# Sums of expert outputs moved behind six of eight weight rows, and the next gather behind the first expert's second layer

## The chip, the cores and the metric

One NeuronCore of a Trainium2 chip runs the whole kernel. The metric is the device time of one execution in microseconds (us). Before the change it is 1108.04 us, the median of 3 runs (1106.1 to 1108.91).

## The reference

One step of a one-layer decoder trunk on 304 tokens (256 prompt tokens, 32 sample tokens, 16 meta tokens). A mixer (RG-LRU, convolution module and gated linear attention side by side, behind one input and one output projection) is followed by a mixture of 32 experts, of which each of the 288 remaining tokens uses four. The change lies in the mixture:

```python
def expert_block(args):
    xb, e = args
    hid = xb @ lp["moe_w1"][e] + lp["moe_b1"][e]          # 1024 x 2048
    gate = jnp.minimum(hid[:, :D_FF], SWIGLU_LIMIT)
    lin = jnp.clip(hid[:, D_FF:], -SWIGLU_LIMIT, SWIGLU_LIMIT)
    act = gate * jax.nn.sigmoid(SWIGLU_ALPHA * gate) * (lin + 1.0)
    return act @ lp["moe_w2"][e] + lp["moe_b2"][e]        # 1024 x 1024
...
rows = out[dest] * gates.reshape(-1)[order][:, None]
y = jax.ops.segment_sum(rows, tok, num_segments=n)
```

The output of the mixture is added to the layer's input and normalised. All data are float32, so the weights of the experts are 12 MiB each, 384 MiB in all.

## The kernel before

The mixer and the routing take the first 173 us. Then the experts run in 16 pairs. Pairs 0 and 1 are the "first" group, pairs 2 to 13 run in a loop, two pairs to an iteration, and pairs 14 and 15 are the "last" group; pair 15 is also called final. Each expert takes up to 64 tokens (the capacity), so the two experts of a pair, called j = 0 and j = 1, share matrices of 128 columns.

**The ring of weights.** SyncE's queue loads the weights into a ring of eight slots of 2 MiB, called pieces here (`load_group`, L492). A pair uses twelve pieces: 12n to 12n+3 for the first layer of j = 0 in pair n, the next four for that of j = 1, then two each for their second layers. In the first and last groups each piece is a DMA of its own; in the loop the first-layer pieces go two by two, as units of 4 MiB. An issue of piece k waits until TensorE has counted `w_used` to k - 7 (`room`, L497; a unit waits for its second piece). TensorE counts `w_used` up behind every second k step of a first layer (L1939) and every fourth of a second layer (L1955), always after one piece.

**TensorE's order in a pair** (`pair`, L1918) is written out by hand:
1. first layer of j = 0 (`first_layer`, L1919; 8 k steps, banks 0 and 1), with the gather of the upper half of the pair's tokens (`gather(1)`, L1890, bank 5) between k = 2 and k = 3;
2. sums 0 and 1 (`combine`, L1898): the outputs of the pair before, `eout`, are spread over the tokens by a matmul with `putT`, into banks 6 and 7. There are five such sums, into banks 6, 7, 5, 2 and 4, and VectorE adds each to the running result (`add_part`, L1390), which counts `y_added`;
3. the biases of j = 1 (`biases`, L1796, matmuls at L1793), which open banks 0 and 1 again and wait until VectorE has read them (`g1_ready`, `l1_ready`, written by L1428 and L1429);
4. sums 2 to 4;
5. first layer of j = 1, with the transposes of j = 0's activations (`inner`, L1957, L1961) between k = 3 and k = 4;
6. the next pair's `gather(0)` into bank 2 and its biases of j = 0; in the final pair two `residual` matmuls (L1915) instead;
7. transposes of `put` (L2009), the matrix that places and weighs the outputs of the pair;
8. second layer of j = 0 (`second_layer`, L1941, matmuls at L1951) with `inner(1)` in its middle, then that of j = 1.

**VectorE's order in a pair**: move the gathered tokens (L1377), build `pick` and `bsel`, activate j = 0 (L1428 to L1434: two reads of the banks, two products), the five additions, `make_put(0)` (L1439), `bsel` (L1324), activate j = 1, `make_put(1)`, move the next gather's result, copy half of the outputs (L1445). ScalarE computes the sigmoid (L918) and copies transposed tiles and the other half of the outputs.

In the code a wait is `eng.wait_ge(semaphore, count)`. An engine works through its own instructions in the order written. The two places around the change, before it:

```python
pe.wait_ge(bsel_ready, 2 * pi + 2)
pe.wait_ge(g1_ready, 2 * pi + 1)
pe.wait_ge(l1_ready, 2 * pi + 1)
biases(1)
```

Of the kernel before, what the change touches and what calls it, by code (L numbers as in the profile page):

```python
# [23 lines left out]
P = 128  # L24
D = 1024
KT = D // P
# [42 lines left out]
NCOMB = 5  # L69
# [48 lines left out]
def build_kernel(nc, x_prompt, x_sample, state_conv_a, state_rglru, state_conv_b, state_gla, meta_tokens, ln0_g, ln0_b,  # L118
# [4 lines left out]
    with ExitStack() as ctx:  # L123
# [14 lines left out]
        ident = sb("ident", [P, P])  # L138
# [125 lines left out]
        put = late(3, 2 * CAP)  # L264
# [40 lines left out]
        bank = [ctx.enter_context(nc.psum_tensor(f"bank{n}", [P, 512], F32)) for n in range(8)]  # L305
# [50 lines left out]
        pick_ready, bsel_ready, put_ready = sem("pick_ready"), sem("bsel_ready"), sem("put_ready")  # L356
        gather_full, xT_ready = sem("gather_full"), sem("xT_ready")
# [602 lines left out]
        def _(dve):  # L960
# [361 lines left out]
            def make_bsel(e, j):  # L1322

                dve.tensor_scalar(bsel[0:2 * NE, j, :], ones[0:2 * NE, 0:CAP], selx[0:2 * NE, bass.ds(e, 1)], None, ALU.mult  # L1324
                                  ).then_inc(bsel_ready, 1)
# [95 lines left out]
            with dve.Fori(0, n_pass) as r:  # L1421
                with dve.Fori(0, NE // GROUP) as g:
                    for q in range(2):
                        pi = r * PAIRS + 2 * g + q
                        def activate(j):
                            n, e = 2 * pi + j, GROUP * g + 2 * q + j
                            dve.wait_ge(w_used, PAIR * pi + W1P * j + W1P)
                            dve.tensor_scalar(g1[:, :], bank[0][:, :], LIMIT, None, ALU.min).then_inc(g1_ready, 1)  # L1428
                            dve.tensor_scalar(l1[:, :], bank[1][:, :], LIMIT, -LIMIT, ALU.min, ALU.max).then_inc(l1_ready, 1)  # L1429
                            dve.wait_ge(l1_ready, n + 1)  # L1430
                            dve.scalar_tensor_tensor(l1[:, :], l1[:, :], 1.0, g1[:, :], ALU.add, ALU.mult).then_inc(t_done, 1)
                            dve.wait_ge(t_done, n + 1)
                            dve.wait_ge(sg_ready, n + 1)
                            dve.tensor_tensor(l1[:, :], l1[:, :], sg[:, :], ALU.mult).then_inc(act_ready, 1)  # L1434

                        def make_put(j):
                            n, e = 2 * pi + j, GROUP * g + 2 * q + j
                            for t in range(3):
                                ins = dve.tensor_scalar(put[:, t, j * CAP:(j + 1) * CAP], io64[:, :], posm[:, t, bass.ds(n, 1)],  # L1439
                                                        gates[:, t, bass.ds(e, 1)], ALU.is_equal, ALU.mult)  # L1440
                            ins.then_inc(put_ready, 1)

                        def expert_out(j):
                            dve.wait_ge(w_used, PAIR * pi + 2 * W1P + 2 * j + 2)
                            dve.tensor_copy(eout[64 * j:64 * j + 64, 1, :], bank[OUT_BANK[j]][64:128, :]).then_inc(out_ready, 1)  # L1445

                        e0 = GROUP * g + 2 * q
                        dve.wait_ge(gather_full, 2 * pi + 5)
                        batch_out(q, 1)
                        make_pick(2 * pi + 2)  # L1450
                        make_bsel(e0 + 1, 1)
                        activate(0)
                        for c in range(NCOMB):
                            add_part(c, NCOMB * pi)
                        make_put(0)
                        make_bsel(e0 + 2, 0)
                        activate(1)
                        make_put(1)
                        dve.wait_ge(gather_full, 2 * pi + 6)
                        batch_out(1 - q, 0)  # L1460
                        expert_out(0)
                        expert_out(1)
# [58 lines left out]
        def _(pe):  # L1521
# [274 lines left out]
            def biases(j):  # L1796

                bias_bank(j, 0)
                bias_bank(j, 1)
# [98 lines left out]
            def combine(pi, c):  # L1898

                out = bank[COMB_BANK[c]]  # L1900
                if c == 0:
                    for q in range(4):
                        ins = pe.matmul(out[SAMP * q:SAMP * q + SAMP, 0:QD], putT[:, 2 * P:2 * P + SAMP],  # L1903
                                        eout[:, q // 2, (q % 2) * QD:(q % 2 + 1) * QD], start=True, stop=True)
                    ins.then_inc(comb_full, 1)
                    return
                t, h = divmod(c - 1, 2)
                pe.matmul(out[:, :], putT[:, t * P:(t + 1) * P], eout[:, h, :], start=True, stop=True).then_inc(comb_full, 1)  # L1908

            def residual(c):  # L1910

                if c == 4:
                    pe.matmul(bank[LAST_BANK[c]][:, 0:QD], ident[:, :], Yq[:, :], start=True, stop=False)
                else:
                    pe.matmul(bank[LAST_BANK[c]][:, :], ident[:, :], Y[:, c // 2, c % 2 * 512:(c % 2 + 1) * 512],  # L1915
                              start=True, stop=False)

            def pair(q, gi, pi, first=False, final=False, group=""):  # L1918
                def first_layer(j, k0, k1):  # L1919

                    for k in range(k0, k1):
                        f = (PAIR * q + W1P * j) // 2 + k // 4
                        if k % 4 == 0:
                            pe.wait_ge(w_full[f % 4], 16 * (gi * 3 + f // 4 + 1))
                        if k % 4 == 2 and group == "first":
                            pe.wait_ge(w_half[f % 4], 16 * (f // 4 + 1))
                        if k % 4 == 2 and group == "last":
                            pe.wait_ge(w1_half_last[f % 4], 16 * (f // 6 + 1))
                        if j == 0 and k < 4 and first:
                            pe.wait_ge(xT_first, k + 1)  # L1930
                        elif j == 0 and k % 4 == 0:
                            pe.wait_ge(xT_ready, 2 * pi + k // 4)
                        for b in range(2):
                            for h in range(2):
                                c = f % 4 * 2 * SLOT + k % 4 * MB1 + (2 * b + h) * 512
                                ins = pe.matmul(bank[b][64 * h:64 * h + 64, :], xT[:, q, k, j * CAP:(j + 1) * CAP],  # L1936
                                                ring[:, c:c + 512], start=False, stop=k == KT - 1)
                        if k % 2 == 1:
                            ins.then_inc(w_used, 1)  # L1939
# [36 lines left out]
                else:  # L1976
                    first_layer(0, 3, KT)

                pe.wait_ge(putT_ready, pi + 1)
                pe.wait_ge(out_ready, 4 * pi + 1)  # L1980
                combine(pi, 0)
                combine(pi, 1)
                pe.wait_ge(bsel_ready, 2 * pi + 2)
                pe.wait_ge(g1_ready, 2 * pi + 1)
                pe.wait_ge(l1_ready, 2 * pi + 1)
                biases(1)
                pe.wait_ge(xT_ready, 2 * pi + 1)
                for c in range(2, NCOMB):
                    combine(pi, c)
                first_layer(1, 0, 4)  # L1990
                inner(0)
                first_layer(1, 4, KT)

                if final:
                    pe.wait_ge(y_added, NCOMB * pi + NCOMB)
                    residual(0)
                    residual(1)
                else:
                    pe.wait_ge(pick_ready, pi + 3)
                    pe.wait_ge(y_added, NCOMB * pi + 4)  # L2000
                    gather(0)
                    pe.wait_ge(bsel_ready, 2 * pi + 3)
                    pe.wait_ge(g1_ready, 2 * pi + 2)
                    pe.wait_ge(l1_ready, 2 * pi + 2)
                    biases(0)
                pe.wait_ge(put_ready, 2 * pi + 2)
                pe.wait_ge(actT_ready, 2 * pi + 1)
                for t in range(3):
                    ins = pe.transpose(bank[3][:, t * P:(t + 1) * P], put[:, t, :], ident[:, :])  # L2009
                    if final and t == 0:  # L2010
                        ins.then_inc(gather_full, 1)
                ins.then_inc(putT_full, 1)
                pe.wait_ge(y_added, NCOMB * pi + NCOMB)
                second_layer(0, 0, 4)
                pe.wait_ge(putT_ready, pi + 2)
                inner(1)
                if final:
                    pe.wait_ge(xT_ready, 2 * pi + 2)
                    residual(4)
                second_layer(0, 4, KT)  # L2020
                pe.wait_ge(actT_ready, 2 * pi + 2)
                second_layer(1, 0, KT)

# [60 lines left out]
```

## Time and profile before

| what | before |
|---|---|
| median of 3 runs | 1108.04 us (1106.1 to 1108.91) |
| the profiled execution | 1106.05 us |
| its span, first to last instruction | 1104.3 us |
| TensorE busy | 1071.1 us (97%) |
| VectorE busy | 374.0 us (34%) |
| ScalarE busy | 163.5 us (15%) |
| moved by DMA | 425.77 MB, 386 GB/s over the span |
| mean granted TensorE clock | 0.993 of full speed |

The page of the profile has the span in 40 slices, each 27.6 us long. In them a digit is the busy share of an engine in tenths. Busy time of TensorE is that of a pipelined engine, so it does not say how fast it works; the timeline (instructions in order of time, those of one line merged) and the windows (busy time, granted clock and DMA rate of a stretch) say more. Matmuls in float32 have two records each. In a row of the timeline, "x24" is the number of records, and the bracket gives idle time of the engine ahead of it and what ended that.

### The profile page before, as it was taken

How to read it: one execution, taken by the hardware profiler on the slowest of the kernel's cores; microseconds unless marked ns; L12 is line 12 of the kernel's file. 1: busy time of each engine (PE TensorE's matmuls, PEld its weight loads, DVE VectorE, ACT ScalarE, POOL GpSimd, SP SyncE). 2: the span in 40 equal slices, each digit the busy share in tenths (PEclk: the TensorE clock that was granted, in tenths of full speed). 3: DMA queues.
4: the chain of work that ended last, by engine and by line, in shares of the span. 5: the costliest groups of instructions: out<-in, count | busy, mean ns of one | idle time of the engine just before them, and what ended most of it. 6: DMA issues, size and time to landing. Idle time of an engine off the chain costs nothing.

```text
span 1104.3 us, 13732 instructions
## 1 busy us (share of the span) xinstructions
PE 1071.1 (97%) x5411; PEld 464.0 (42%) x5411; DVE 374.0 (34%) x939; ACT 163.5 (15%) x314; POOL 44.2 (4%) x103
## 2 busy tenths in 40 slices
PE   7999999999999999999999999999999999999996
PEld 4667554434333343334333333333334343434332
DVE  4797665313131414141413122323231312222134
ACT  4264633000000010001000101010101010010002
POOL 8000210000000000000000000000000000000001
PEclk9999999999999999999999999999999999999998
DMA  9533549999999999999999999999999999999993
GB/s 297 197 151 160 232 166 358 402 426 426 414 439 425 431 433 428 430 432 431 425 438 424 434 429 434 427 436 425 434 428 434 432 431 430 424 429 427 427 428 150
DMA packets 34878, 425.77 MB, mean 386 GB/s; under 512 B 5865, under 2 KB 12398, under 8 KB 16409
## 3 DMA queue, kind: packets, MB, share of 16 engines
q1 hardware_dynamic: 32961, 423.62, 91.1%
q0 software_dynamic: 1888, 1.75, 0.6%
q8 instruction: 20, 0.33, 0.1%
q14 instruction: 9, 0.07, 0.0%
HBM read 423.39 MB, written 2.17 MB: 385 GB/s over the span
## 4 chain that ended last, share of the span: by engine, by line
PE 76%; DMA 21%; DVE 2%; issue 0%; ACT 0%; SPq 0%; DVEq 0%
PE bank L1936 36%; DMA ring<-in_moe_w_dram 21%; PE bank L1951 10%; PE bank L1536 7%; PE bank L1895 6%; PE bank L1908 6%; PE bank L1763 3%; PE bank L1793 2%; PE bank L1563 1%; PE bank L1961 1%; PE bank L1541 1%; PE bank L1903 1%; PE bank L1785 0%; PE bank L2009 0%; PE bank L1756 0%
## 5 line engine op out<-in xcount | busy, mean ns | idle before, releaser
L1936 PE MATMUL bank<-ring,hT 128*64 128x512 f32 x2048 | 457.2, 599 | 12.6 <-DMA ring<-in_moe_w_dram 12.5
L1936 PEld LDWEIGHTS bank<-ring,hT 128*64 128x64 f32 x2048 | 143.2, 137 | 297.8 <-issue 282.8
L1951 PE MATMUL bank<-ring 128*64 128x512 f32 x1024 | 226.8, 595 | 0.0
L1428 DVE TENSOR_SCALAR ring<-bank 128x512 f32<-128x512 f32 x32 | 22.1, 691 | 311.8 <-PE bank L1936 311.8
L1951 PEld LDWEIGHTS bank<-ring 128*64 128x64 f32 x1024 | 70.7, 137 | 132.8 <-issue 130.6
L1445 DVE COPY ring<-bank 64x512 f32<-64x512 f32 x32 | 22.2, 694 | 218.9 <-PE bank L1951 218.9
L1895 PEld LDWEIGHTS bank<-ring 128*128 128x128 f32 x744 | 85.4, 192 | 25.1 <-issue 25.1
L1895 PE MATMUL bank<-ring 128*128 128x128 f32 x744 | 91.3, 279 | 0.0
L1377 DVE TENSOR_SCALAR hT<-bank,ring 128x128 f32<-128x128 f32 x128 | 43.6, 401 | 129.7 <-PE bank L1895 129.3
L918 ACT ACTIVATE ring<-ring 128x512 f32<-128x512 f32 x32 | 20.1, 629 | 379.3 <-DVE ring L1428 379.3
L1908 PE MATMUL bank<-ring 128*128 128x512 f32 x128 | 63.5, 618 | 0.0
L922 ACT ACTIVATE ring<-bank 128x512 f32<-128x512 f32 x32 | 19.1, 597 | 248.4 <-PE bank L1961 248.4
L1536 PE MATMUL bank<-hT,ring 128*128 128x304 f32 (+1 forms) x208 | 55.1, 424 | 0.0
L1390 DVE TENSOR_TENSOR xt<-xt,bank 128x512 f32<-128x512 f32 x64 | 43.9, 685 | 5.8 <-PE bank L1908 5.5
L1536 PEld LDWEIGHTS bank<-hT,ring 128*128 128x128 f32 x208 | 40.1, 195 | 13.2 <-issue 0.4
L933 ACT ACTIVATE ring<-bank 64x512 f32<-64x512 f32 x32 | 18.9, 589 | 148.8 <-PE bank L1951 148.8
L667 POOL TENSOR_TENSOR ring<-ring 128x256 f32<-128x256 f32 x1 | 0.7, 722 | 943.1 <-ACT ring L946 943.1
L1908 PEld LDWEIGHTS bank<-ring 128*128 128x128 f32 x128 | 21.7, 189 | 34.9 <-issue 34.9
L1793 PE MATMUL bank<-ring 32*64 32x512 f32 x256 | 35.9, 613 | 0.0
L1763 PE MATMUL bank<-ring 128*128 128x512 f32 x64 | 29.2, 602 | 0.0
L1961 PEld LDWEIGHTS bank<-ident,ring 128*128 128x128 f32 x128 | 18.0, 210 | 26.0 <-issue 26.0
L1439 DVE TENSOR_SCALAR ring<-io,ring 128x64 f32<-128x64 f32 x96 | 24.1, 307 | 0.0
(327 smaller groups left out, 616.8 us busy)
## 6 DMA issues: line engine op xcount, KB each, us to landing
ring<-in_moe_w_dram SPq DMA_DIRECT2D x96, 2048.0 KB, 28.4
ring<-in_moe_w_dram SPq DMA_DIRECT2D x48, 4096.0 KB, 27.6
ring<-in_w_in_dram SPq DMA_DIRECT2D x5, 1536.0 KB, 13.5
ring<-in_w_out_dram SPq DMA_DIRECT2D x2, 2048.0 KB, 10.9
ring<-in_w_in_dram SPq DMA_DIRECT2D x1, 2048.0 KB, 13.3
xt<-in_x_prompt_dram SPq DMA_DIRECT2D x2, 512.0 KB, 3.7
lnbc<-in_ln_g_dram SPq DMA_DIRECT2D x2, 512.0 KB, 12.2
lnbc<-in_ln_b_dram SPq DMA_DIRECT2D x2, 512.0 KB, 12.5
```

Source lines behind the costliest of these rows:

```text
L1377: ins = dve.tensor_scalar(xT[:, parity, 4 * b + k, :], bank[(2, 5)[b]][:, k * 2 * CAP:(k + 1) * 2 * CAP], ln1c[:, 0, 4 * b + k:4 * b + k + ...
L1390: dve.tensor_tensor(dst, dst, bank[COMB_BANK[c]][:, :], ALU.add).then_inc(y_added, 1)
L1439: ins = dve.tensor_scalar(put[:, t, j * CAP:(j + 1) * CAP], io64[:, :], posm[:, t, bass.ds(n, 1)], gates[:, t, bass.ds(e, 1)], ALU.is_equa ...
L1445: dve.tensor_copy(eout[64 * j:64 * j + 64, 1, :], bank[OUT_BANK[j]][64:128, :]).then_inc(out_ready, 1)
L1536: ins = pe.matmul(out, a, b, start=n == 0, stop=n == len(pairs) - 1)
L1763: ins = pe.matmul(bk(f"P{t}{c}")[:, :], yT[:, k, cols[t][0]:cols[t][1]], wout[:, k, c * 512:(c + 1) * 512], start=k == 0, stop=k == KT - 1)
L1793: pe.matmul(bank[b][64 * h:64 * h + 64, :], bsel[e0:e0 + NE, j, :], b1_sb[e0:e0 + NE, h, :], start=True, stop=False)
L1895: ins = pe.matmul(out, xh[:, t, k * P:(k + 1) * P], pick[:, t, :], start=t == 0, stop=t == 2)
L1908: pe.matmul(out[:, :], putT[:, t * P:(t + 1) * P], eout[:, h, :], start=True, stop=True).then_inc(comb_full, 1)
L1936: ins = pe.matmul(bank[b][64 * h:64 * h + 64, :], xT[:, q, k, j * CAP:(j + 1) * CAP], ring[:, c:c + 512], start=False, stop=k == KT - 1)
L1951: ins = pe.matmul(bank[OUT_BANK[j]][64 * h:64 * h + 64, :], actT[:, j, k % 4, (k // 4) * CAP:(k // 4 + 1) * CAP], ring[:, c:c + 512], star ...
L1961: ins = pe.transpose(bank[3][:, k * P:(k + 1) * P], l1[:, k:512:4], ident[:, :])
```

## The change

On VectorE, `make_put(1)` moves ahead of the activation of j = 1. On TensorE, in every pair but the final one, all five sums move behind k = 5 of the first layer of j = 1, as one run; in the final pair they stay where they were. In the first group (pairs 0 and 1) the transposes of `put` move into the middle of the first half of j = 0's second layer, and the next pair's `gather(0)` and biases move from ahead of j = 0's second layer to behind it. No instruction that computes is added or dropped.

```diff
                         for c in range(NCOMB):
                             add_part(c, NCOMB * pi)
                         make_put(0)
+                        make_put(1)
                         make_bsel(e0 + 2, 0)
                         activate(1)
-                        make_put(1)
                         dve.wait_ge(gather_full, 2 * pi + 6)
...
-                pe.wait_ge(putT_ready, pi + 1)
-                pe.wait_ge(out_ready, 4 * pi + 1)
-                combine(pi, 0)
-                combine(pi, 1)
+                def combined(c0, c1):
+                    if c0 == 0:
+                        pe.wait_ge(putT_ready, pi + 1)
+                        pe.wait_ge(out_ready, 4 * pi + 1)
+                    else:
+                        pe.wait_ge(xT_ready, 2 * pi + 1)
+                    for c in range(c0, c1):
+                        combine(pi, c)
+
+                late_sums = not final
+                if not late_sums:
+                    combined(0, 2)
                 pe.wait_ge(bsel_ready, 2 * pi + 2)
                 pe.wait_ge(g1_ready, 2 * pi + 1)
                 pe.wait_ge(l1_ready, 2 * pi + 1)
                 biases(1)
+                if not late_sums:
+                    combined(2, NCOMB)
                 pe.wait_ge(xT_ready, 2 * pi + 1)
-                for c in range(2, NCOMB):
-                    combine(pi, c)
                 first_layer(1, 0, 4)
                 inner(0)
-                first_layer(1, 4, KT)
...
+                if late_sums:
+                    first_layer(1, 4, 6)
+                    combined(0, 2)
+                    combined(2, NCOMB)
+                    first_layer(1, 6, KT)
                 else:
+                    first_layer(1, 4, KT)
...
+                if group == "first":
+                    pe.wait_ge(y_added, NCOMB * pi + NCOMB)
+                    pe.wait_ge(actT_ready, 2 * pi + 1)
+                    second_layer(0, 0, 2)
+                    put_over()
+                    second_layer(0, 2, 4)
+                else:
+                    if final:
+                        pe.wait_ge(y_added, NCOMB * pi + NCOMB)
+                        residual(0)
+                        residual(1)
+                    else:
+                        next_gather()
+                    put_over()
+                    pe.wait_ge(y_added, NCOMB * pi + NCOMB)
+                    second_layer(0, 0, 4)
                 pe.wait_ge(putT_ready, pi + 2)
                 inner(1)
...
                 second_layer(0, 4, KT)
+                if group == "first":
+                    next_gather()
                 pe.wait_ge(actT_ready, 2 * pi + 2)
                 second_layer(1, 0, KT)
```

`next_gather()` holds the waits, `gather(0)` and `biases(0)` of step 6 as they were, and `put_over()` the waits and transposes of step 7.

## Rows read from the trace of the kernel before

**Rows 1.** The page, section 2: busy tenths in 40 slices.
```profile
PE   7999999999999999999999999999999999999996
...
DMA  9533549999999999999999999999999999999993
```

**Rows 2.** Windows: us, busy time by engine, clock, DMA share, GB/s.
```profile
199.00:202.00 3.00, 3.00 (x18) 1.00 (x15) 0.00 (x0) 0.00 (x0) 0.00 (x0) 1.00 0.61 180
...
260.00:262.00 2.00, 2.00 (x10) 0.68 (x12) 0.00 (x0) 0.60 (x1) 0.00 (x0) 1.00 1.05 336
...
480.00:1080.00 600.00, 585.76 (x2923) 229.88 (x2921) 154.62 (x381) 49.95 (x79) 0.00 (x0) 0.99 1.00 430
...
686.00:688.00 2.00, 2.00 (x6) 0.53 (x6) 0.00 (x0) 0.00 (x0) 0.00 (x0) 0.50 1.10 475
```

**Rows 3.** Timeline of TensorE, pair 1: start us, us, line, operation, records.
```profile
229.94 5.32 PE L1936 MATMUL bank<-ring,hT 128*64 128x512 f32 x24
...
246.79 0.64 PE L1903 MATMUL bank<-ring 128*32 128x256 f32 x8
247.36 1.12 PE L1908 MATMUL bank<-ring 128*128 128x512 f32 x2
248.42 1.09 PE L1793 MATMUL bank<-ring 32*64 32x512 f32 x8
249.44 2.84 PE L1908 MATMUL bank<-ring 128*128 128x512 f32 x6
252.21 7.09 PE L1936 MATMUL bank<-ring,hT 128*64 128x512 f32 x32
...
266.93 2.94 PE L1895 MATMUL bank<-ring 128*128 128x128 f32 x24
...
285.92 1.46 PE L1936 MATMUL bank<-ring,hT 128*64 128x512 f32 x6
```

**Rows 4.** Waits of TensorE: total us, times, longest us.
```profile
PE bank L1936 <- DMA ring<-in_moe_w_dram: 12.5, 8, 2.2
```

**Rows 5.** Timeline of TensorE, pair 15.
```profile
1030.23 3.65 PE L1936 MATMUL bank<-ring,hT 128*64 128x512 f32 x16
1035.04 1.94 PE L1936 MATMUL bank<-ring,hT 128*64 128x512 f32 x8 [1.16 <-DMA ring<-in_moe_w_dram]
...
1072.23 0.55 PE L2009 MATMUL bank<-ident,ring 128*128 128x128 f32 x3 [1.60 <-DVE ring L1439]
1072.71 3.65 PE L1951 MATMUL bank<-ring 128*64 128x512 f32 x16
...
1087.85 1.12 PE L1915 MATMUL bank<-xt,ident 128*128 128x512 f32 x2
```

**Rows 6.** Timeline of TensorE's weight loads, the last piece in use.
```profile
1083.98 0.14 PEld L1951 LDWEIGHTS bank<-ring 128*64 128x64 f32 x2 [0.38 <-DMA ring<-in_moe_w_dram]
```

**Rows 7.** Timeline of SyncE's DMA queue: issues of pieces 12, 18, (24, 25) and (26, 27).
```profile
199.93 0.33 SPq L514 DMA_DIRECT2D ring<-in_moe_w_dram  x1
...
226.71 0.33 SPq L514 DMA_DIRECT2D ring<-in_moe_w_dram  x1
...
259.49 0.35 SPq L510 DMA_DIRECT2D ring<-in_moe_w_dram  x1
...
267.17 12.57 SPq L510 DMA_DIRECT2D ring<-in_moe_w_dram  x2
```

**Rows 8.** Timeline of VectorE in pair 1: the two reads, a put.
```profile
246.91 0.69 DVE L1428 TENSOR_SCALAR ring<-bank 128x512 f32<-128x512 f32 x1 [6.24 <-PE bank L1936]
247.52 0.68 DVE L1429 TENSOR_SCALAR ring<-bank 128x512 f32<-128x512 f32 x1
...
252.92 0.76 DVE L1439 TENSOR_SCALAR ring<-io,ring 128x64 f32<-128x64 f32 x3
```

**Rows 9.** Timeline of TensorE behind two waits for weights.
```profile
684.21 5.35 PE L1936 MATMUL bank<-ring,hT 128*64 128x512 f32 x16 [2.25 <-DMA ring<-in_moe_w_dram]
...
917.91 5.37 PE L1936 MATMUL bank<-ring,hT 128*64 128x512 f32 x24 [2.23 <-DMA ring<-in_moe_w_dram]
```

More of the change, by code:

```diff
@@ L1986, in pair, with next_gather @@
                 biases(1)
+                if not late_sums:
+                    combined(2, NCOMB)
                 pe.wait_ge(xT_ready, 2 * pi + 1)
-                for c in range(2, NCOMB):
-                    combine(pi, c)
                 first_layer(1, 0, 4)
                 inner(0)
-                first_layer(1, 4, KT)
[L1994 to L1997, printed above, removed]
-                else:
+                if late_sums:
[3 more added lines that the diff above has]
+                    first_layer(1, 6, KT)
+                else:
+                    first_layer(1, 4, KT)
+                def next_gather():
                     pe.wait_ge(pick_ready, pi + 3)
@@ L2005, in pair, with put_over @@
                     biases(0)
[L2006 to L2014, printed above, removed]
+                def put_over():
+                    pe.wait_ge(put_ready, 2 * pi + 2)
+                    pe.wait_ge(actT_ready, 2 * pi + 1)
+                    for t in range(3):
+                        ins = pe.transpose(bank[3][:, t * P:(t + 1) * P], put[:, t, :], ident[:, :])
+                        if final and t == 0:
+                            ins.then_inc(gather_full, 1)
+                    ins.then_inc(putT_full, 1)
+                if group == "first":
+                    pe.wait_ge(y_added, NCOMB * pi + NCOMB)
+                    pe.wait_ge(actT_ready, 2 * pi + 1)
+                    second_layer(0, 0, 2)
[11 more added lines that the diff above has]
+                    second_layer(0, 0, 4)
                 pe.wait_ge(putT_ready, pi + 2)
```

## The prediction

> **What bounds the kernel now.** I read the slices of the page first: from slice 9 on TensorE and the DMA engines both stand at 9 tenths, so both are nearly full and the question is which one waits for the other [rows 1]. The stretches say it in numbers: 430 GB/s from 480 to 1080 us, and a hole before that, 180 GB/s from 199 to 202 us [rows 2]. A piece of weights is 2.097 MB, so at 430 GB/s it takes 4.88 us and the twelve pieces of a pair 58.5 us. The timeline of TensorE gives its own pace: pair 1 begins at 229.94 us and pair 2 at 285.92 us, 55.98 us with no idle time between them [rows 3]. So TensorE is the faster of the two by 2.5 us a pair. It first lives on the lead that the ring gave; in the second half it waits for weights, 8 times for 12.5 us in all, 2.2 us at most [rows 4]. From there the stream of weights sets the pace, and the end is the start of the stream, plus its bytes over its rate, plus its holes, plus the tail behind the last piece. The last piece lands at 1083.98 us, and the last second layer is done at 1087.85 us [rows 5, 6].
>
> **The holes of the stream.** The DMA queue issues a piece when a slot of the ring is free, that is when TensorE has signalled the matmuls that used it. The hole at 199 to 202 us ends with the issue of piece 12 at 199.93 us, which waits for k = 0 and 1 of expert 1's first layer in pair 0 [rows 7]. It is worth 3 x (430 - 180) / 430 = 1.74 us, so the piece before ended, counted like an issue (the latency to the first byte drops out of the differences), at 198.19. From 199.93 twelve pieces reach 258.5, and the next unit (24, 25) is issued at 259.49: 1.0 us dry. Two units later the second of the two issues that take 12.57 us from 267.17 on starts at about 279.4, where the stream is due at 279.0: 0.4 us [rows 7]. My sum is 3.1 us of holes; the stretch from 260 to 262 us shows 2 x (430 - 336) / 430 = 0.44 us where I have 1.0, so half a microsecond is what such a sum can be off by [rows 2]. After that the queue only gets longer.
>
> **The change, part by part.**
> (a) The sums move. Between the first layer of expert 0 (ends 246.79) and that of expert 1 (begins 252.21) stand today: sums 0 and 1, 1.63 us; the biases, 1.02; sums 2 to 4, 2.77 [rows 3]. In all pairs but the last the 4.40 us of sums go between k = 5 and k = 6 of expert 1's first layer. No matmul is added or removed.
> (b) What sums 0 and 1 cover. The biases of expert 1 overwrite banks 0 and 1 and wait until VectorE has read them. Those two reads start at 246.91 and end at 248.20 [rows 8]. Today that lies under sums 0 and 1, which end at 248.42. With the sums gone TensorE stands still from 246.79 until shortly behind 248.20; a release takes about 0.1 us (VectorE begins 0.12 behind TensorE's end), I take 248.26, so **1.47 us in each of 15 pairs**. The bounds: 0 if the wait were covered otherwise (nothing else is queued in front of it), 1.63 if it cost all that the sums filled. I take 1.47, which comes from two rows.
> (c) The split of the eight k steps into 6 and 2 adds a break. A run of 16 records of the layer takes 3.65 us and one of 32 takes 7.09, so a break costs up to 0.21; joining sum 1 and sums 2 to 4 into one run gives back as much (two records take 1.12, six take 2.84, so the four added cost 0.43 each, and eight 3.70, not 3.96) [rows 3, 5]. Between -0.2 and +0.2 a pair; I take 0. So a pair takes 55.98 + 1.47 = 57.45 us, still under 58.5.
> (d) Earlier room. The signals for k = 1, 3 and 5 of expert 1 come 4.40 - 1.47 = 2.93 us earlier, all later ones of the pair 1.47 us later.
> (e) VectorE. The five additions follow the sums by one; the second put is now built before the activation of expert 1 and not behind it. The adds end 0.9 us behind the sums, the two puts and the selection need 1.8 more (0.76 a put), and two k steps of matmuls last half of 7.09 us [rows 3, 8]: nothing on TensorE waits for them, and the activation begins as before. In the last pair this pays: there TensorE waits 1.60 us for the put, which stands behind the whole activation [rows 5]. That wait goes; next late would be the data.
> (f) The first group. Its second layer begins ahead of the gather and the biases (3.89 us), so the room from expert 0's second layer comes about 4 us earlier, less the 1.47 of (b), and that from expert 1's at +1.47. The gather reads nothing that is late, and the move of its result to the other buffer ends some 3 us before pair 1 or 2 reads it. No DMA changes its place in the queue.
>
> **The stream summed again**, all counted like issues. Piece 12 is issued at 199.93 - 2.93 = 197.0, before 198.19: no hole, 1.74 us gained. (Pieces not named come in time.) Piece 18 is due at 198.19 + 6 x 4.88 = 227.5 and issued at 226.71 + 1.47 = 228.2: 0.7 dry. Unit 24 is due at 257.5 and issued at 259.49 + 1.47 - 2.93 = 258.0: 0.6. Unit 26 is due at 267.8, but waits for the end of expert 1's first layer in pair 1, which is two bubbles late: 267.17 + 2.94 = 270.1, 2.3 dry [rows 7]. Unit 40, in pair 2, is due at 338.4 and issued 49.5 + 1.47 behind the pair's start (288.86), at 339.8: 1.4 dry. After it the queue grows by 1.1 us a pair. Holes 5.0 against 3.1: **the stream ends 1.9 us later**; the last piece lands at 1085.9, and with 3.87 us behind it the second layer is done at 1089.7.
>
> **TensorE summed again.** Pair 2 begins at 288.86, pair 15 at 288.86 + 13 x 57.45 = 1035.7 instead of 1030.23. Data in time: pair 13 begins at 920.8, and its weights, for which it waited until 917.91 today, are there by 919.8 [rows 9]. In the last pair 57.62 us (to 1087.85) lose the wait of 1.16 for data and that of 1.60 for the put: 54.86, so 1090.6, or 1089.9 if (c) gives back 0.05 a pair [rows 5]. TensorE now ends 2.1 to 2.75 us later, the stream 1.9. I take **+2.4 us**: 1108.5 for a profiled execution of 1106.05, and 1110.4 on the median of 1108.04. The profiled one lies 2 us under the median, within the spread of the three runs. What a measurement of this kernel can tell from no change is about 0.3%, 3.3 us, so this counts as no difference.
>
> **Rivals.**
> R1, the clock of TensorE falls behind the bubbles; slower. After a wait of 2.25 us at 684 us the granted clock stood at 0.50 (1.2 GHz) from 686 to 688, and 16 records took 5.35 us instead of 3.65, 1.70 us lost; after one of 2.23 at 918 us 24 records took 5.37 us, as 24 do in pair 1 (5.32), so the clock stayed at 2.4 GHz [rows 2, 3, 5, 9]. The shorter wait of 1.60 us left the 16 records behind it at 3.65 us [rows 5]. If it fell in every pair, 57.45 + 1.70 = 59.15 is over 58.5 and TensorE is some 25 us late, 1135; in half of them +12, 1122. Chance 0.08. The Trainium skill speaks against the change here: "TensorE: Matmul & The Clock Gate", section "A second HAM failure mode: psum-queue depth-cycling", says that small idle times between groups of matmuls, when frequent, make the clock swing between its levels. By that rule the time would be R1's. This trace agrees with it only for one wait of 2.25 us; the one of 1.60 does not bear it out.
> R2, the bubble is the mechanism but longer, or the added break is not paid back; slower. There is no slack: every 0.1 us a pair is 1.3 us at the end, and from 0.07 us more a pair the total is over 3.3 us. With 0.2 (the upper end of c): 13 x 0.2 = 2.6 on top, 1113. Chance 0.23.
> R3, the stream alone sets the end, TensorE is some tenths a pair quicker than summed: +0.5 to +1.9, 1109.2. Chance 0.19; with my forecast's 0.40 it shares the verdict.
> R4, a gain. The hole at 200 us goes and the bubbles cost the stream nothing, because the latency before data hides 1 or 2 us: -1.74, and 0.4 at the end, 1106. Chance 0.10, of which 0.06 for over 0.3%: there is less idle time in the stream (3.1 us) than that would take.
>
> **How the numbers follow.** Slower by over 0.3%: R1 and most of R2, 0.30. Faster by over 0.3%: 0.06. Within: 0.64. The range reaches from R4's 1106 to just beyond R2, 1114.5; R1 is left out.
>
> **What the profile would show.** TensorE idle about 1.5 us in front of the biases (L1793) in 15 pairs, released by VectorE's L1429; a pair start every 57.4 us; waits for weights nearly gone (12.5 us before); no wait of 1.6 us for the put at the end; the hole at 199 to 202 us gone, new ones near 270 and 340 us. I would be wrong if pairs still started every 58.4 us with waits for weights (R3, R4), or if the clock row showed 0.5 behind the bubbles (R1).

## The result, and the profile after

The changed kernel takes 1117.87 us (median of 4 runs, 1116.95 to 1120.55), beside 1107.35 us for the kernel before, which was run once more with it. The ratio is 1.0097, with a 95% interval of 1.0079 to 1.0115: **slower by about 1%, some 10 us.** The forecast was 1110.4 us and a range up to 1114.5.

| what | before | after |
|---|---|---|
| profiled execution | 1106.05 us | 1116.95 us |
| its span | 1104.3 us | 1114.1 us |
| mean granted TensorE clock | 0.993 | 0.989 |
| TensorE's waits for weights | 12.5 us, 8 times | none |
| its waits in front of the biases of j = 1 | none | 22.2 us, 15 times |

First the waits of TensorE (total, times, longest), which answer to [rows 4]:

```profile
PE bank L1793 <- DVE ring L1429: 22.2, 15, 1.5
PE bank L1541 <- DMA ring<-in_ln_b_dram: 6.3, 1, 6.3
PE bank L1541 <- ACT xt L692: 1.6, 2, 1.2
PE bank L1785 <- ACT hT L864: 0.3, 1, 0.3
```

One kind of wait has taken the place of the other. L1429 is VectorE's second read of the banks. Next TensorE's timeline of pair 1 and of the start of pair 2, beside [rows 3]:

```profile
239.68 8.80 PE L1936 MATMUL bank<-ring,hT 128*64 128x512 f32 x40
249.96 1.09 PE L1793 MATMUL bank<-ring 32*64 32x512 f32 x8 [1.48 <-DVE ring L1429]
250.98 7.09 PE L1936 MATMUL bank<-ring,hT 128*64 128x512 f32 x32
258.00 0.75 PE L1961 MATMUL bank<-ident,ring 128*128 128x128 f32 x4
258.68 3.65 PE L1936 MATMUL bank<-ring,hT 128*64 128x512 f32 x16
262.26 0.64 PE L1903 MATMUL bank<-ring 128*32 128x256 f32 x8
262.83 3.70 PE L1908 MATMUL bank<-ring 128*128 128x512 f32 x8
...
289.19 5.32 PE L1936 MATMUL bank<-ring,hT 128*64 128x512 f32 x24
```

The bubble is 1.48 us long, the five sums stand between k = 5 and 6, and pair 2 begins at 289.19 us, 3.3 us later than before. From here 13 pairs of 57.48 us would reach pair 15 at 1036.4. It begins later:

```profile
1043.27 5.32 PE L1936 MATMUL bank<-ring,hT 128*64 128x512 f32 x24
...
1080.26 1.98 PE L1915 MATMUL bank<-xt,ident 128*128 128x512 f32 x4
1082.08 0.49 PE L2024 MATMUL bank<-ident,ring 128*128 128x128 f32 x3
1082.50 3.65 PE L1951 MATMUL bank<-ring 128*64 128x512 f32 x16
...
1087.20 10.52 PE L1951 MATMUL bank<-ring 128*64 128x512 f32 x48
1097.66 1.12 PE L1915 MATMUL bank<-xt,ident 128*128 128x512 f32 x2
```

Pair 15 is 13.04 us late against [rows 5] and then wins 3.23 us back (54.39 us instead of 57.62: no wait for data, no wait for the put). The second layer is done 9.81 us late, which is the whole difference of the spans. The 6.8 us between 1036.4 and 1043.27 are in rows like these, TensorE behind two of the 15 bubbles, and two windows (us, busy time by engine, granted clock, DMA share, GB/s) at the first:

```profile
422.57 1.09 PE L1793 MATMUL bank<-ring 32*64 32x512 f32 x8 [1.48 <-DVE ring L1429]
423.59 8.77 PE L1936 MATMUL bank<-ring,hT 128*64 128x512 f32 x32
...
654.20 1.09 PE L1793 MATMUL bank<-ring 32*64 32x512 f32 x8 [1.48 <-DVE ring L1429]
655.21 8.78 PE L1936 MATMUL bank<-ring,hT 128*64 128x512 f32 x32
```

```profile
422.00:426.00 4.00, 3.43 (x14) 1.00 (x16) 1.81 (x3) 0.49 (x1) 0.00 (x0) 0.70 1.03 438
424.00:426.00 2.00, 2.00 (x6) 0.47 (x4) 0.00 (x0) 0.00 (x0) 0.00 (x0) 0.50 1.04 442
```

32 records of the first layer take 8.77 us and not 7.09, and the granted clock is 0.50 from 424 to 426 us: it has fallen to 1.2 GHz, and later it comes back to 2.4. In windows of 2 us over the whole stretch of the experts falls of the clock begin at 422, 654, 828 and 1002 us, each time directly behind a bubble. The shortfall adds up to 6.84 us, and the four pairs in question are 59.2 us long instead of 57.5. Before, there were two falls, behind waits for weights at 684 and 801 us. The rows of [rows 9] have the first; this is the second, where 24 records take 7.07 us and not 5.32:

```profile
801.05 7.07 PE L1936 MATMUL bank<-ring,hT 128*64 128x512 f32 x24 [2.23 <-DMA ring<-in_moe_w_dram]
```

They cost the kernel nothing: TensorE had time in hand there, and the pairs that begin at 684.21 and 801.05 us are 58.41 and 58.43 us long, like those beside them (58.43 and 58.44).

The stream of weights, beside [rows 2]:

```profile
199.00:202.00 3.00, 3.00 (x18) 1.21 (x16) 0.00 (x0) 0.60 (x1) 0.00 (x0) 1.00 1.02 437
...
262.00:280.00 18.00, 18.00 (x87) 7.27 (x86) 7.33 (x16) 2.31 (x4) 0.00 (x0) 1.00 0.93 383
338.00:344.00 6.00, 6.00 (x30) 2.01 (x28) 0.69 (x1) 0.59 (x1) 0.00 (x0) 1.00 0.88 341
```

The hole at 200 us is gone. The missing rate is that below 430 GB/s: one hole of 18 x 47 / 430 = 2.0 us has come near 270 us, and one of 6 x 89 / 430 = 1.2 us near 340 us, where the forecast had 2.3 and 1.4.

### The profile page after: what moved, and what is told of

Read it like the earlier page. It is cut to its first block, busy times and chain, and to the rows that moved or that the text cites. A ratio compares the mean times of both kernels' runs of the same rounds, so it can differ in the third digit from the quotient of the medians.

```text
span 1114.1 us, 13742 instructions
## 1 busy us (share of the span) xinstructions
PE 1073.1 (96%) x5411; PEld 466.1 (42%) x5411; DVE 377.8 (34%) x939; ACT 164.1 (15%) x314; POOL 44.3 (4%) x103
## 4 chain that ended last, share of the span: by engine, by line
PE 96%; DVE 2%; issue 1%; DMA 0%; ACT 0%; DVEq 0%
PE bank L1936 41%; PE bank L1951 20%; PE bank L1895 8%; PE bank L1536 7%; PE bank L1908 5%; PE bank L1793 3%; PE bank L1763 3%; PE bank L1961 2%; PE bank L1563 1%; DVE ring L1429 1%; PE bank L1541 1%; PE bank L1903 1%; PE bank L2024 1%; PE bank L1785 0%; PE bank L1756 0%
## 5 line engine op out<-in xcount | busy, mean ns | idle before, releaser
L1936 PE MATMUL bank<-ring,hT 128*64 128x512 f32 x2048 | 463.3, 603 | 0.0
L1445 DVE COPY ring<-bank 64x512 f32<-64x512 f32 x32 | 22.2, 693 | 208.7 <-PE bank L1951 208.7
L1386 DVE TENSOR_TENSOR ring<-ring,bank 128x256 f32<-128x256 f32 x16 | 6.7, 421 | 182.3 <-PE bank L1903 182.3
L1908 PE MATMUL bank<-ring 128*128 128x512 f32 x128 | 59.5, 606 | 0.0
L1793 PE MATMUL bank<-ring 32*64 32x512 f32 x256 | 35.8, 611 | 22.2 <-DVE ring L1429 22.2
L1536 PEld LDWEIGHTS bank<-hT,ring 128*128 128x128 f32 x208 | 39.1, 190 | 12.5 <-issue 0.4
L1763 PE MATMUL bank<-ring 128*128 128x512 f32 x64 | 29.2, 601 | 0.0
## 6 DMA issues: line engine op xcount, KB each, us to landing
lnbc<-in_ln_g_dram SPq DMA_DIRECT2D x2, 512.0 KB, 12.5
```

The source lines that it names most:

```text
L1536: ins = pe.matmul(out, a, b, start=n == 0, stop=n == len(pairs) - 1)
L1763: ins = pe.matmul(bk(f"P{t}{c}")[:, :], yT[:, k, cols[t][0]:cols[t][1]], wout[:, k, c * 512:(c + 1) * 512], start=k == 0, stop=k == KT - 1)
L1793: pe.matmul(bank[b][64 * h:64 * h + 64, :], bsel[e0:e0 + NE, j, :], b1_sb[e0:e0 + NE, h, :], start=True, stop=False)
```

## The experiments

Nine kernels ran, one of them in two sets (cover and cover_again), in five rounds each beside the kernel before. The kernel before had medians of 1106.3 to 1106.7 us in those. "Falls" are stretches of the profiled execution with a granted clock under 1, from 180 us to the end of the last second layer (some 8 us or more behind it, in the last microseconds, the clock is at 0.50 in every kernel). The mean granted clock of a whole execution, which each run has, says that the profiled executions are no exceptions: 0.985 to 0.989 in the four of the changed kernel, 0.986 to 0.990 in late_only, 0.984 to 0.989 in split_bias, but 0.992 to 0.996 in the 12 of fill and 0.992 to 0.997 in the 11 of half_fill.

| label | usual pair, us | idle before the biases, us | falls | median us | ratio to before (95%) |
|---|---|---|---|---|---|
| before | 55.98 | none | 2 | 1106.5 | 1 |
| the change | 57.48 | 1.48 | 4 | 1117.87 | 1.0097 (1.0079 to 1.0115) |
| fill | 57.53 | none | 0 | 1109.64 | 1.0027 (1.0016 to 1.0039) |
| half_fill | 57.49 | 0.85 | 0 | 1109.05 | 1.0025 (1.0012 to 1.0038) |
| late_only | 57.49 | 1.48 | 4 | 1118.47 | 1.0112 (1.0094 to 1.0131) |
| split_bias | 57.38 | 0.89 | 4 | 1116.29 | 1.0090 (1.0072 to 1.0109) |
| half_cover | 56.92 | 0.92 | 0 | 1107.73 | 1.0004 (0.9991 to 1.0018) |
| cover | 56.13 | none | 0 | 1105.25 | 0.9987 (0.9976 to 0.9999) |
| cover_again | 56.13 | none | 1 | 1105.32 | 0.9990 (0.9978 to 1.0001) |
| cover_old_first | 56.13 | none | 1 | 1106.38 | 0.9998 (0.9987 to 1.0009) |
| put_only | 55.98 | none | 2 | 1106.02 | 0.9997 (0.9985 to 1.0008) |
| first_only | 55.98 | none | 3 | 1108.89 | 1.0019 (1.0005 to 1.0033) |

The usual pair is the distance between the starts of two pairs where TensorE waits for no weights and the clock stays up.

**Work in the bubble.** Against the changed kernel:

```diff
                 if not late_sums:
                     combined(0, 2)
+                else:
+                    pe.wait_ge(putT_ready, pi + 1)
+                    pe.wait_ge(out_ready, 4 * pi + 1)
+                    pe.matmul(bank[3][:, :], ident[:, :], xh[:, 0, 0:512], start=True, stop=True)
+                    pe.matmul(bank[3][:, 0:320], ident[:, :], xh[:, 0, 0:320], start=True, stop=True)
```

Expected:

> The changed kernel, with two matmuls that nobody reads (512 and 320 columns of the normalised rows against the identity, into bank 3) in front of the biases of expert 1 in the 15 pairs that have the bubble. They last about 1.4 us, so TensorE works through the time in which it otherwise waits 1.48 us for VectorE; the pair stays as long as it is, 57.5 us. Theory (the bubble of 1.48 us makes TensorE the only bound, +2.75 us, and the granted clock falls behind some of these idle times, four times 1.7 us in the profiled run): the clock stays at full in every pair, pair 15 starts near 1036.5 us, the run takes 1109.5 to 1111, some 7 us less than the changed kernel. Rival (the clock falls for another reason, such as the run of sums inside the layer or the time of day of the fall, and idle time has no part in it): still four or so falls, 1117 to 1118.

Measured: 1109.64 us. Useless work in the place of idle time, and some 8 us are gone. TensorE's timeline in pair 1:

```profile
252.02 1.12 PE L1995 MATMUL bank<-ring,ident 128*128 128x512 f32 x2
252.98 0.70 PE L1996 MATMUL bank<-ring,ident 128*128 128x320 f32 x2
253.61 1.09 PE L1793 MATMUL bank<-ring 32*64 32x512 f32 x8
```

(This execution begins pair 1 at 235.16 us, 3.6 us later than the changed kernel: in the mixer, ahead of 180 us, its clock lost 5.1 us and not 1.7. It also waits 1.4 us for weights near the end. So its total of 1114.78 us is over the median, and pair 15 starts at 1042.2 us, not near 1036.5.) The pair is as long as with the bubble, and no window between 180 and 1096 us has a clock under 1. So the pair's length and the clock are separate costs, and the clock's falls come with the idle time. The rival, that idle time has no part in them, is refuted: the run of sums inside the layer is there in fill too.

**Half of the bubble filled.** As above, but one matmul of 256 columns instead of the two.

> The changed kernel with one matmul that nobody reads (256 columns of the normalised rows against the identity, bank 3, about 0.5 us) in front of the biases of expert 1 in 15 pairs: the pair stays 57.5 us long, since VectorE's reads decide when the biases start, but TensorE's idle time is about 0.9 to 1.0 us in place of 1.48. Theory (half_cover had no falls because its idle time is 0.9 us next to full-array work, and split_bias had four because its idle time of 0.9 us is followed by 1.5 us of bias matmuls instead of 1.0): no falls, 1109 to 1111, as with the full filling. Rival (a pair paced by TensorE falls with any idle time of about 0.9 us; half_cover was spared by chance): four falls, 1116 to 1118.

Measured: 1109.05 us, no falls. The waits of TensorE:

```profile
PE bank L1793 <- DVE ring L1429: 12.8, 15, 0.9
PE bank L1541 <- DMA ring<-in_ln_b_dram: 6.6, 1, 6.6
```

15 waits of 0.85 us, 57.49 us a pair, and the clock stays up. Pair 15 begins at 1035.91 us, and the last second layer is done at 1090.30. Here TensorE is the bound just as in the changed kernel, so the pace of a pair does not make the falls.

**Sums 0 and 1 back in their place.** Against the changed kernel:

```diff
-                if not late_sums:
-                    combined(0, 2)
+                combined(0, 2)
...
                     first_layer(1, 4, 6)
-                    combined(0, 2)
                     combined(2, NCOMB)
```

> The changed kernel with sums 0 and 1 put back in front of the biases of expert 1 in every pair; sums 2 to 4 stay behind k = 5, the first group and the earlier put stay as changed. Theory (all of the loss is the bubble that these two sums had covered): no wait of L1793 for L1429, pairs of 56.0 us until TensorE meets the stream of weights, then 58.4 us as before, and the holes of the stream near 200, 260 and 280 us mostly gone: 3 us less than the kernel before at best, 1104 to 1107. Rival (the loss comes from the late sums 2 to 4, the broken layer or the first group's new order): 1110 or more.

Measured: 1105.25 us, and in a second set of runs 1105.32. It undoes the whole loss. The waits of TensorE are again those for weights:

```profile
PE bank L1936 <- DMA ring<-in_moe_w_dram: 12.1, 12, 1.7
PE bank L1541 <- DMA ring<-in_ln_b_dram: 6.1, 1, 6.1
PE bank L1541 <- ACT xt L692: 2.0, 2, 1.5
PE bank L1951 <- DMA ring<-in_moe_w_dram: 1.8, 2, 1.1
```

The second set:

> The kernel with sums 0 and 1 in front of the biases, sums 2 to 4 late, new first group and early put, once more, to narrow its interval. Theory (it gains 0.4 us from the end of the stream and some tenths from fewer holes): 0.9985 to 0.9995 of the kernel before. Rival (no gain, the first measurement was low by chance): 1.000.

Both sets lie about 0.1% under the kernel before. One interval ends at 0.9999, the other at 1.0001, so the gain is between none and 0.24% and is only just told from none. The 3 us that it could have been at best did not come: the hole at 200 us is gone, but from 262 to 280 us the stream makes 406 GB/s, 18 x 24 / 430 = 1.0 us short.

**Sum 0 alone in its place.** Against the changed kernel, `combined(0, 2 if final else 1)` stands in front of the biases, and sum 1 goes with the late ones.

> The changed kernel with sum 0 alone in front of the biases of expert 1, sums 1 to 4 late. The wait for L1429 should be 1.48 - 0.57 = 0.9 us, the pair 56.9 us. Theory: under the pace of the stream, so the length of the pair no longer counts; with two or fewer falls of the clock 1105 to 1108. Rival (the clock falls as often behind 0.9 us of idle time as behind 1.48): falls in four pairs or so, 6.8 us against the 1.5 us a pair that TensorE then has in hand, so they are mostly absorbed too, but they show in the windows.

Measured: 1107.73 us, 0.92 us idle, no falls; TensorE reaches the pace of the weights late, in pair 10, and waits for them 4 times, 5.4 us. No difference from the kernel before.

**The biases bank by bank.** Against the changed kernel:

```diff
                 pe.wait_ge(g1_ready, 2 * pi + 1)
+                bias_bank(1, 0)
                 pe.wait_ge(l1_ready, 2 * pi + 1)
-                biases(1)
+                bias_bank(1, 1)
```

> The changed kernel; only the biases of expert 1 are opened one bank at a time: the bias of bank 0 as soon as VectorE has read bank 0 (L1428), that of bank 1 after L1429. All sums stay late. Theory (the loss is the length of the wait in front of the biases, by its sum and by the clock): the wait of 1.48 us becomes one of about 0.87 and one of about 0.1 us, a pair takes 57.5 - 0.5 = 57.0 us, the stream of weights sets the end again, falls of the clock are rarer or gone: 1105 to 1109. Rival (the late sums themselves cost, or any idle time there lets the clock fall): 1113 or more.

Measured: 1116.29 us, which is the number of the rival. TensorE's timeline in pair 7, one of the four pairs with a fall:

```profile
595.19 1.58 PE L1793 MATMUL bank<-ring 32*64 32x512 f32 x8 [0.89 <-DVE ring L1428]
596.70 8.78 PE L1936 MATMUL bank<-ring,hT 128*64 128x512 f32 x32
```

And its weight loads for the biases of bank 1:

```profile
595.69 0.19 PEld L1793 LDWEIGHTS bank<-ring 32*64 32x64 f32 x4 [0.31 <-DVE ring L1429]
```

The idle time did shrink to 0.89 us, but the biases now take 1.51 us (595.19 to 596.70) instead of 1.02, so that the pair is only 0.1 us shorter, not 0.5. The rows show where the forecast of 0.5 us went. Bank 1's biases still wait for L1429, until 595.69, and the first layer begins at 596.70: the four records of one bank take 1.0 us, as long as the eight of both banks do in the changed kernel (1.02). So the first layer begins 1.0 us behind L1429 in either kernel. That the two banks overlap there because their biases use different rows of the array (32 each) is argued from the code, not tested. The falls are as many as behind 1.48 us. Idle time alone therefore does not tell them: 0.85 us with a full matmul ahead and biases of 1.02 us behind gave none, 0.91 us with sum 0 ahead and the same biases (half_cover) gave none, 0.89 us with biases of 1.51 us behind gave four. Waits for weights have full-width matmuls on both sides. In cover, cover_again and cover_old_first 16 of them last 1.74 us, longer than the bubble, and two have a fall behind them; in before, put_only and first_only 13 last 2.05 to 2.25 us, and six have one. So length counts, and it is not all that counts; these are counts from single executions.

**Each part alone, on the kernel before.** The late sums, with nothing else of the change:

> The kernel before with only the five sums moved behind k = 5 of expert 1's first layer, in every pair but the last; put and the first group as before. Theory: 15 bubbles of 1.48 us and some falls of the clock, and the wait of 1.6 us for the put in the last pair is back: 1118 to 1121. Rival (the first group's new order or the put carries part of the loss): 1110 to 1115.

Measured: 1118.47 us. The bubble and the falls are there, and the last pair's wait for the put is back:

```profile
PE bank L1793 <- DVE ring L1429: 22.3, 15, 1.5
PE bank L1541 <- DMA ring<-in_ln_b_dram: 6.2, 1, 6.2
PE bank L1541 <- ACT xt L692: 1.8, 2, 1.4
PE bank L2024 <- DVE ring L1439: 1.6, 1, 1.6
```

So the late sums alone make the loss. `make_put(1)` ahead of the activation, alone:

> The kernel before with only the put of expert 1 built ahead of its activation on VectorE. Theory (before, the stream of weights sets the end; the last pair's wait of 1.6 us for the put goes, but the last piece lands at 1084.0 as before): second layer done at most 0.4 us earlier, 1107 to 1108 beside 1107.4 for the kernel before. Rival (the last pair is bound by TensorE and not by data): 1.6 us earlier, 1105.8.

Measured: 1106.02 us, no difference. The wait for the put goes and one for the last piece takes its place, ahead of the last 16 records of the last second layer:

```profile
1084.31 3.65 PE L1951 MATMUL bank<-ring 128*64 128x512 f32 x16 [1.16 <-DMA ring<-in_moe_w_dram]
```

The second layer is done at 1087.90 us, before at 1087.85, so the rival's 1.6 us did not come. The new order of the first group, alone (`late_sums = False` and the old place of `make_put(1)` in the changed kernel):

> The kernel before with the new order of the first group alone (pairs 0 and 1: second layer of expert 0 around the put's transposes, gather and biases behind it); sums and the put as before. Theory (the stream sets the end, the hole at 200 us comes from a signal that this part does not touch): hole still there, 1106 to 1108, no difference. Rival (this part is what helps or hurts the stream): 2 us or more off.

Measured: 1108.89 us, 0.2% slower: the theory of no difference missed, and the number is that of the rival. The put comes too late for its new place inside the second layer when it is built behind the activation:

```profile
210.72 1.89 PE L1951 MATMUL bank<-ring 128*64 128x512 f32 x8
214.41 0.55 PE L2024 MATMUL bank<-ident,ring 128*128 128x128 f32 x3 [1.80 <-DVE ring L1439]
214.89 3.48 PE L1951 MATMUL bank<-ring 128*64 128x512 f32 x8
```

TensorE stands still for 1.80 us, and behind it the clock falls (8 records in 3.48 us, not 1.89), one of the three falls of this execution. A second such wait follows in pair 1, and pair 2 begins at 291.41 us instead of 285.92. This part of the change needs the early put. With it and the covered biases, the old order of the first group:

> The kernel with sums 0 and 1 in front of the biases, sums 2 to 4 late and the early put, but the first group in the order of before. Theory (its gain comes from the earlier room of the late sums 2 to 4 and the put, not from the first group): 1104.5 to 1106, as with the new first group. Rival (the first group's order gives the gain): 1106.5 to 1107.5.

Measured: 1106.38 us, 0.9998. With the new order it was 0.9987 and 0.9990. It lies between the theory's 1104.5 to 1106 and the rival's 1106.5 to 1107.5, and the intervals overlap, so which part brings the tenth of a per cent stays open.

## Why the prediction was wrong, point by point

**What was right.** Step (b), the bubble: 1.47 us in 15 pairs was forecast, 1.48 us in 15 pairs came. Step (c), the length of a pair: 57.45 us forecast, 57.48 measured; the extra break is paid back by the joined sums (3.70 us for eight records). Steps (d) and (f): piece 12 was issued at 197.04 us (197.0), piece 18 at 228.33 (228.2). Step (e): the put no longer stops TensorE in the last pair, and nothing waits for VectorE's additions. The sum for TensorE without the clock is borne out by the kernels without falls. It had pair 15 begin at 1035.7 us and the last second layer done at 1089.9 to 1090.6, 2.1 to 2.75 us later; half_fill has 1035.91 and 1090.30. The ratios of fill and half_fill, 1.0027 and 1.0025, are 2.8 to 3.0 us. The waits for weights vanished, as they had to when TensorE became the slower of the two.

**The step that failed** is "TensorE summed again". It adds 13 pairs of 57.45 us and the last pair, and has no term for the clock: the falls stood only in R1, at a chance of 0.08, and R1 was left out of the range. In its place the profiled execution shows four falls behind 15 bubbles, at the price that R1 itself had, 1.70 us each, 6.84 us in all; they carry pair 15 from 1036.4 to 1043.27 us. The medians agree: 1.0097 minus the 1.0026 of the filled kernels is 0.7%, some 8 us. The profiled execution, with a mean clock of 0.989, is the fastest of the four; the others have 0.985 to 0.988.

Three things were read too lightly. The evidence for safety was one wait of 1.60 us without a fall; with 4 falls in 15, one wait without a fall says next to nothing. (It came again without a fall in late_only and first_only, so the row was no accident, but it did not stand for the bubble.) That wait was followed by transposes and then full-width work, while the new bubble is followed by the biases, which use 32 rows of the array each, for another 1.02 us; half_fill, half_cover and split_bias fit with such surroundings counting, but no run tests them alone. And the trace before was not read to the end: R1 names one fall, behind 2.25 us, and says that the trace bears the clock's swing out for that wait only. The wait of 2.23 us at 801.05 us has a fall too, so it was two falls behind four waits of over 2 us. R1 was then priced only for falls in all or half of the pairs, not for a few.

The Trainium skill's rule that R1 named ("TensorE: Matmul & The Clock Gate", section "A second HAM failure mode: psum-queue depth-cycling") pointed the right way: short idle times that come often make the clock swing. The changed kernel's trace agrees with it in four of 15 pairs, and no fall came in the other eleven.

**Why the time lies above the range.** The forecast noted that TensorE had no slack left, and summed only its own rows. In the kernel before, two falls of 1.7 us cost nothing, because TensorE was 2.5 us a pair faster than the weights. The bubble took 1.5 us of that margin, and TensorE no longer waited for weights anywhere; so each of the four falls went into the total in full.

## What to carry to other kernels

A short piece of work between the last matmul into a bank and the first that overwrites it covers the other engine's read; before moving it, ask what fills the time. The idle time on TensorE had two prices here, its own length (some 3 us in the total) and the falls of the clock (some 8 us). A filler of useless matmuls is a cheap experiment that tells them apart: here it kept the length of a pair and took away only the falls.

## What the runs showed that was not expected

The falls come with a pattern: in late_only they lie at 422, 596, 770 and 946 us, three pairs apart, in split_bias at 422, 596, 712 and 886 us, three, two and three pairs apart. The same bubble stands in every pair, and most pairs are spared; which pair is hit stays open. Some 0.6 us of full-array matmul in front of the bubble (half_fill) was enough to end them in the profiled execution. Splitting two biases that cover different rows of the array lengthened them from 1.02 to 1.51 us, and an idle time cut from 1.48 to 0.89 us won 0.1 us a pair.
